# Gather order in a routed expert layer: V rows behind U rows, query products and index products

## The chip, the cores and the metric

The kernel runs on one core of a Trainium2 chip. The metric is the time on the device in microseconds (us), lower is better. Five engines run side by side, each through its own instructions in order, and wait for one another by semaphores: TensorE (matrix products; PE in the profile), VectorE (DVE), ScalarE (ACT), GpSimd (POOL) and SyncE (SP). In this kernel GpSimd issues the indirect DMA gathers and SyncE the plain loads.

## The reference

Two networks in a row on 256 tokens of width 1024. The first has two layers; each is a mixer (attention and pooling) and then the expert part, which is all that the change touches:

```python
def one_block(xblk):                      # 128 tokens
    q = (xblk @ w_query).reshape(B, TOKEN_BLOCK, N_PEER_HEADS, 2, SUBKEY_DIM)
    s = jnp.einsum('bthpd,hpnd->bthpn', q, sub_keys).astype(jnp.float32)
    vals, idx = lax.top_k(s, PEER_TOPK)
    cand = ...                            # 16 x 16 sums of the two halves
    top_s, pos = lax.top_k(cand, PEER_TOPK)
    eidx = jnp.take_along_axis(cand_idx, pos, axis=-1)
    g = jax.nn.softmax(top_s, axis=-1).astype(xblk.dtype)
    u = expert_u[eidx]
    h = jnp.einsum('btd,bthkd->bthk', xblk, u)
    act = jax.nn.gelu(h, approximate=False) * g
    return jnp.einsum('bthk,bthkd->btd', act, expert_v[eidx])
```

There are 8 heads, 16 experts per token and head, and 16384 experts, each with a row of 1024 floats in U and one in V. Every layer so reads 256 x 8 x 16 rows of U and as many of V, 268 MB in all. The second network (four dense layers) is not touched.

## The kernel before, in words

**Chunks.** A chunk is one head for one tile of 128 tokens; there are 16 (NCH), in the order of CHUNKS: heads 0 and 1 on tile 0, heads 0 and 1 on tile 1, then heads 2 to 7, each on tile 0 and tile 1. Chunk 4 is the first of head 2, chunk 8 the first of head 4.

**GpSimd** (line 2767 on) issues the gathers, one queue, strictly in order. `u_rows(c, g)` gathers group g of chunk c: four DMAs of 128 rows (512 KB each) into four of 8 buffers; it waits for the chunk's expert indices and for the dots that free the buffers (two groups back). `v_rows(q)` gathers set s = q % 4 of chunk c = q // 4, also four DMAs, into buffers that belong to the set; it waits until TensorE has summed the same set of the chunk before (`v_free`), and set 0 also for the chunk's indices by pair (`it_used`). U groups and V sets alternate: V set q follows U group q + VLAG, VLAG = 2. V rows are laid out by pair: a DMA takes the rows of 8 x 16 pairs of token and expert, not of one expert place for 128 tokens, and so needs its indices in another order than U.

**VectorE** (line 2385 on) works through `dots(c)`: 16 dots of a token's row with a U row (line 2454), about 1.15 us each. Between them it makes the expert lists of a later chunk, in four parts (`topk_part`): part 0 copies the head's scores out of PSUM (lines 2390, 2394), part 3 ends with the indices (line 2429) and with "indices spread" (line 2433, semaphore `ri_ready`), from which TensorE makes the indices by pair. From chunk 3 on, the dots of chunk c carry the parts of chunk c + 2, part 3 behind the last dot. The start differs: the dots of chunk 1 carry the parts of chunk 2 (behind dots 8 and 12), and the dots of chunk 2 carry those of chunk 3 (parts 0 and 1 behind dot 4, parts 2 and 3 behind dot 8) and of chunk 4 (behind dots 12 and 16). At the end of a chunk's dots VectorE spreads the weights (line 2466), copies the indices by pair of the next chunk (`take_indices`, line 2443), and then `stationaries(c)` (line 2479) writes the columns of expert weights that TensorE uses as stationary operand ("columns" below, semaphore `wst_ready`). Then come the dots of chunk c + 1.

**TensorE** (line 1073 on) does per chunk: `weights_by_pair` (line 1126, "weights product"), then `expert_sum(c)`: four sets of V rows times the columns (line 1141), each waiting for its rows to land. The product for the indices by pair of chunk c + 2 (`indices_by_pair`, line 1118, "index product", waits for `ri_ready`) lies ahead of set 2. Into six of the chunks (ASKED: chunk to head) the work on a later head is woven: `query_keys` (line 1084, "keys": four transposes of the head's sub keys, behind the copy of the scores of the head before, and in chunk 1 behind the copy at line 2390), `query_rows` parts 0 to 3 (line 1097, two halves of 16 products in the code, 32 in the trace) and `key_scores` (line 1108, "scores"). Before: keys ahead of the columns of set 0 (in chunk 1 behind set 0), parts 0 and 1 behind set 0, parts 2, 3 and scores behind set 1.

**ScalarE** copies keys and query halves out of PSUM between two chunks' gates. **SyncE** loads the query weights of head h (2 MB) when the query of head h - 2 is done.

## Time and profile before

| | us |
|---|---|
| median of 3 runs | 3297.96 |
| lowest and highest | 3285.51, 3304.04 |
| span of the profiled execution | 3263.7 |

The time of the profiled execution itself is not listed beside the three; its span, from the first to the last instruction, is 34.3 us below the median. Shares of the span are averages over stages of different kind: the expert part of layer 0 lies between about 241 us (first gather) and 1019 us, that of layer 1 between about 1230 us and 2008 us, and the rest is dense work. In rows of the trace, the first number is the start in us, the second how long it took, then engine, line, operation, tiles and count; in brackets is the idle time of the engine just before and what ended it. "issue" means that the profile shows nothing that was waited for, "remote" a releaser that it doesn't know. A product of TensorE has two records where the data are 32-bit floats, so a set of 8 products reads x16. Its ends are modelled, and a record may lie well ahead of the release that follows from it.

### The profile page before, as it was taken

To read this page: it belongs to the slowest core of one execution; us is meant where nothing else is said; L and a number is where in the kernel's file an instruction comes from. 1 tells how busy PE (TensorE), PEld (TensorE's weight loads), DVE (VectorE), ACT (ScalarE), POOL (GpSimd) and SP (SyncE) were. 2 spreads that over 40 slices of the span, in tenths; PEclk is the share of its full clock that TensorE was granted. 3 is DMA by queue.
4 is the path that set the end of the run, shared out by engine and by line. 5 is a ranking of instruction groups with operands and counts; after the bars stand their busy time and mean duration, and the time that the engine had idled before them with its cause. 6 is when DMAs were issued, how large, how long until landed. Compare 5 with 4: busy or idle time off the path is not lost.

```text
span 3263.7 us, 34887 instructions
## 1 busy us (share of the span) xinstructions
PE 2431.9 (75%) x12607; PEld 1727.6 (53%) x12607; DVE 2088.5 (64%) x4416; ACT 933.8 (29%) x1486; POOL 1043.1 (32%) x1060
## 2 busy tenths in 40 slices
PE   5996555544546997555545545999999999999998
PEld 4754422221103764422221102789879988997797
DVE  7878576666656958576666654655555555556654
ACT  3511011110112421011101112544554446445543
POOL 0105566666663105566566663100010001000000
PEclk9998777766667998677666766989999999999999
DMA  9858999999999839999999998345534542554353
GB/s 363 299 209 332 353 374 380 378 379 365 361 378 341 295 139 342 350 370 394 377 359 372 356 365 307 131 143 191 180 130 155 180 168 82 190 194 155 110 193 123
DMA packets 308642, 886.31 MB, mean 272 GB/s; under 512 B 22824, under 2 KB 32144, under 8 KB 308240
## 3 DMA queue, kind: packets, MB, share of 16 engines
q0 software_dynamic: 147456, 536.94, 42.9%
q1 hardware_dynamic: 161040, 347.51, 29.9%
q8 instruction: 82, 1.34, 0.2%
q14 instruction: 64, 0.52, 0.0%
HBM read 883.32 MB, written 1.05 MB: 271 GB/s over the span
## 4 chain that ended last, share of the span: by engine, by line
PE 46%; issue 31%; DVE 9%; another core or an unknown queue 6%; DMA 4%; SPq 2%; ACT 2%; POOL 1%; DVEq 0%; ACTq 0%; POOLq 0%
PE lin L837 7%; PE lin L838 7%; PE lin L839 7%; PE psT L839 2%; PE psT L838 2%; PE psS L838 2%; PE psS L839 2%; PE psT L837 2%; PE psS L837 2%; PE lin L1141 2%; PE psS L1097 2%; PE psS L887 2%; DMA ring<-in_w_in 2%; PE lin L1014 1%
## 5 line engine op out<-in xcount | busy, mean ns | idle before, releaser
L2454 DVE CUSTOM_DVE_ANT_0 proj<-proj,psT 128x1024 f32<-128x1024 f32 x512 | 606.1, 1218 | 211.1 <-DMA proj<-in_expert_u,eidx 120.5
L1928 DVE TENSOR_TENSOR weights_split<-ring,weights_split 128x1024 fp32r<-128x1024 f32 (+1 forms) x360 | 431.5, 1207 | 376.2 <-ACT weights_split L1712 373.6
L2787 POOL DMA_INDIRECT proj<-in_expert_u,eidx x512 | 481.5, 940 | 424.7 <-DVEq L2430 212.7
L1712 ACT ACTIVATE weights_split<-ring 128x1024 fp32r<-128x1024 f32 (+1 forms) x376 | 391.5, 1046 | 467.7 <-PE lin L839 291.6
L1141 PE MATMUL lin<-vbuf,rowb 128*32 128x512 f32 x1024 | 252.0, 879 | 266.8 <-issue 180.4
L2823 POOL TENSOR_TENSOR weights_split<-ring,weights_split 128x1024 fp32r<-128x1024 f32 x16 | 37.9, 2376 | 995.3 <-ACT weights_split L1712 995.3
L1141 PE MATMUL lin<-ring,rowb 128*32 128x512 f32 x896 | 208.8, 755 | 153.1 <-issue 107.1
L837 PE MATMUL lin<-weights_split,xT_high 128*128 128x512 f32 (+1 forms) x736 | 295.0, 401 | 19.6 <-issue 8.2
L839 PE MATMUL lin<-weights_split,xT_high 128*128 128x512 f32 (+1 forms) x736 | 288.1, 391 | 0.0
L2800 POOL DMA_INDIRECT ring<-in_expert_v,pT x224 | 211.0, 942 | 231.4 <-remote 86.8
L2800 POOL DMA_INDIRECT vbuf<-in_expert_v,pT x256 | 241.2, 942 | 115.5 <-issue 76.5
L1141 PEld LDWEIGHTS lin<-vbuf,rowb 128*32 128x32 f32 x1024 | 45.3, 136 | 422.5 <-issue 320.6
L1644 ACT ACTIVATE gel<-hdot 128x16 f32<-128x16 f32 x32 | 6.9, 215 | 771.3 <-DVE hdot L2454 450.1
L1097 PE MATMUL psS<-xT,ring 128*128 128x256 f32 x768 | 197.3, 415 | 32.8 <-issue 22.3
L1097 PEld LDWEIGHTS psS<-xT,ring 128*128 128x128 f32 x768 | 158.5, 210 | 93.3 <-issue 58.0
L837 PE MATMUL lin<-weights_split,act_split 128*128 128x512 f32 x512 | 200.1, 391 | 0.0
L838 PE MATMUL lin<-weights_split,act_split 128*128 128x512 f32 x512 | 199.5, 390 | 0.0
L839 PE MATMUL lin<-weights_split,act_split 128*128 128x512 f32 x512 | 199.2, 389 | 0.0
L1141 PEld LDWEIGHTS lin<-ring,rowb 128*32 128x32 f32 x896 | 39.4, 128 | 284.2 <-issue 226.7
L838 PE MATMUL lin<-weights_split,xT_low 128*128 128x512 f32 (+1 forms) x480 | 186.8, 389 | 0.0
L837 PEld LDWEIGHTS lin<-weights_split,xT_high 128*128 128x128 f32 x736 | 142.5, 194 | 55.5 <-issue 21.1
L839 PEld LDWEIGHTS lin<-weights_split,xT_high 128*128 128x128 f32 x736 | 142.5, 194 | 29.0
(336 smaller groups left out, 4943.9 us busy)
## 6 DMA issues: line engine op xcount, KB each, us to landing
ring<-in_mlp_w_up SPq DMA_DIRECT2D x32, 2048.0 KB, 8.1
ring<-in_mlp_w_down SPq DMA_DIRECT2D x32, 2048.0 KB, 7.9
ring<-in_w_in SPq DMA_DIRECT2D x14, 2048.0 KB, 14.1
ring<-in_w_query SPq DMA_DIRECT2D x14, 2048.0 KB
vbuf<-in_ada_w SPq DMA_DIRECT2D x12, 2048.0 KB, 12.9
ring<-in_diff_w_in SPq DMA_DIRECT2D x11, 2048.0 KB, 8.1
proj<-in_ada_w SPq DMA_DIRECT2D x24, 512.0 KB, 5.1
ring<-in_moba_w_in SPq DMA_DIRECT2D x6, 2048.0 KB, 8.0
```

The source lines that it names most:

```text
L837: pe.matmul(out_ap, lhs[0], rhs[0], start=first, stop=False, skip_group_check=True)
L838: pe.matmul(out_ap, lhs[1], rhs[0], start=False, stop=False, skip_group_check=True)
L839: return pe.matmul(out_ap, lhs[0], rhs[1], start=False, stop=last, skip_group_check=True)
L887: mm = pe.matmul(psS[:, g % 2, t * S:t * S + n], qkT[lo:hi, qb, t * P:(t + 1) * P], qkT[lo:hi, kb, 0:n], start=True, stop=True)
L1097: mm = pe.matmul(psS[:, 1, (b % 2) * S:(b % 2 + 1) * S], query_weights(h)[:, k, b * P:(b + 1) * P], xT[:, k, :], start=(k == 0), stop=(k = ...
L1141: mm = pe.matmul(lin[32 * b:32 * b + 32, 2 * half + t, :], wst[:, c % 2, 4 * b + s, :], vrow(SETROWS * s + b)[:, half * 512:(half + 1) * 5 ...
L1712: act.activation(part(p, 0, kind, w), raw_piece(slot, p, kind, w), ACT.Copy).then_inc(hi_ready, 1)
L1928: dve.tensor_tensor(part(p, 1, kind, w), raw_piece(slot, p, kind, w), part(p, 0, kind, w).bitcast(F32), ALU.subtract).then_inc(lo_ready, 1)
L2454: dve.tensor_tensor_reduce(ubuf[:, n % GB, :], ubuf[:, n % GB, :], x_row, 1.0, 0.0, ALU.mult, ALU.add, hdot[:, cb, k:k + 1]).then_inc(h_re ...
L2787: pool.indirect_dma_start(out=ubuf[:, (16 * c + k) % GB, :], out_offset=None, in_=table["u"], in_offset=bass.IndirectOffsetOnAxis(ap=eidx[ ...
L2800: pool.indirect_dma_start(out=vrow(SETROWS * s + b), out_offset=None, in_=table["v"], in_offset=bass.IndirectOffsetOnAxis(ap=eidxT[:, c % ...
L2823: pool.tensor_tensor(part(p, 1, "flat", D), raw_piece(o_slot, p, "flat", D), part(p, 0, "flat", D).bitcast(F32), ALU.subtract).then_inc(lo ...
```

## The change

Four edits, all in the order of work; no product, copy or DMA is added or removed.

1. `indices_by_pair(c + 2)` goes from ahead of set 2 to ahead of set 0, in chunks 1 to 13.
2. ASKED: heads 4 to 7 are worked on in chunks 3, 5, 7, 9 in place of 4, 6, 8, 10. In these the keys, parts 0 and 1 lie behind set 1, and parts 2, 3 and scores behind set 2. In chunks 1 and 2 (heads 2 and 3) keys, parts 0 and 1 lie behind set 0 and the rest behind set 1; so for chunk 2 only the keys move, from ahead of set 0 to behind it.
3. V rows follow the U rows by three groups for chunks 4 to 14, and by two as before for chunks 0 to 3 and 15.
4. The call of `query_keys` outside `expert_sum` goes.

```diff
-ASKED = {1: 2, 2: 3, 4: 4, 6: 5, 8: 6, 10: 7}
+ASKED = {1: 2, 2: 3, 3: 4, 5: 5, 7: 6, 9: 7}
+LAGS = [2] * (2 * NT) + [3] * (NCH - 2 * NT - 1) + [2]
...
                     pe.wait_ge(wst_ready, c + 1)
+                    if 0 < c < NCH - 2:
+                        indices_by_pair(c + 2)
                     for s in range(NSET):
-                        if s == 2 and 0 < c < NCH - 2:
-                            indices_by_pair(c + 2)
...
-                        if c in ASKED and s < 2:
-                            if c == 1 and s == 0:
+                        if c in ASKED:
+                            if s == (0 if c < 3 else 1):
                                 query_keys(ASKED[c])
-                            query_rows(ASKED[c], 2 * s)
-                            query_rows(ASKED[c], 2 * s + 1)
-                            if s == 1:
+                                query_rows(ASKED[c], 0)
+                                query_rows(ASKED[c], 1)
+                            if s == (1 if c < 3 else 2):
+                                query_rows(ASKED[c], 2)
+                                query_rows(ASKED[c], 3)
                                 key_scores(ASKED[c])
...
                     weights_by_pair(c)
-                    if c in ASKED and c > 1:
-                        query_keys(ASKED[c])
                     expert_sum(c)
...
+                q = 0
+                for c in range(NCH):
                     for g in range(4):
                         u_rows(c, g)
-                        if 4 * c + g >= VLAG:
-                            v_rows(4 * c + g - VLAG)
+                        while q < NSET * NCH and q + LAGS[q // NSET] <= 4 * c + g:
+                            v_rows(q)
+                            q += 1
```

TensorE's order in chunk 1 of a layer, before: the weights product (line 1126), set 0 (vbuf), keys, half of the query, set 1 (ring), the other half, scores, and only then the index product (line 1118).

```order
L1126 MATMUL psS<-const,pT 128x16 [waits indices_by_pair_copied,weights_spread]
L1141 MATMUL lin<-vbuf,rowb 32x512 [waits v_set_landed0,expert_weight_columns_ready]
L1141 MATMUL lin<-vbuf,rowb 32x512 x7
L1084 MATMUL psS<-const,ring 128x128 [waits peer_query_copied,sub_keys_copied,first_tile_scores_copied,sub_keys_loaded0]
L1084 MATMUL psS<-const,ring 128x128 x3
L1097 MATMUL psS<-xT,ring 128x256 [waits sub_keys_copied,query_slot_loaded1]
L1097 MATMUL psS<-xT,ring 128x256 x15
L1141 MATMUL lin<-ring,rowb 32x512 [waits v_set_landed1]
L1141 MATMUL lin<-ring,rowb 32x512 x7
L1097 MATMUL psS<-xT,ring 128x256 [waits peer_query_copied]
L1097 MATMUL psS<-xT,ring 128x256 x15
L1108 MATMUL psS<-pT,sm 128x128 [waits peer_query_copied]
```

The same place now; the lines are one or more further on in the file (1127 is the weights product, 1119 the index product).

```order
L1127 MATMUL psS<-const,pT 128x16 [waits indices_by_pair_copied,weights_spread]
L1119 MATMUL psS<-const,pT 128x16 [waits indices_spread,expert_weight_columns_ready]
L1142 MATMUL lin<-vbuf,rowb 32x512 [waits v_set_landed0]
L1142 MATMUL lin<-vbuf,rowb 32x512 x7
L1085 MATMUL psS<-const,ring 128x128 [waits peer_query_copied,sub_keys_copied,first_tile_scores_copied,sub_keys_loaded0]
L1085 MATMUL psS<-const,ring 128x128 x3
L1098 MATMUL psS<-xT,ring 128x256 [waits sub_keys_copied,query_slot_loaded1]
L1098 MATMUL psS<-xT,ring 128x256 x15
L1142 MATMUL lin<-ring,rowb 32x512 [waits v_set_landed1]
```

The index product, with its wait for the spread indices, stands ahead of set 0 and of all that follows it.

GpSimd's order at the start of chunk 4, now (proj is a U group, ring, pr and vbuf are V sets; each group is one row with its waits and one for the other three DMAs).

```order
L2788 DMA proj<-in_expert_u,eidx 128x1024 [waits expert_dots_ready]
L2788 DMA proj<-in_expert_u,eidx 128x1024 x3
L2801 DMA vbuf<-in_expert_v,pT 128x1024 [waits v_set_free]
L2801 DMA vbuf<-in_expert_v,pT 128x1024 x3
L2788 DMA proj<-in_expert_u,eidx 128x1024 [waits expert_dots_ready]
L2788 DMA proj<-in_expert_u,eidx 128x1024 x3
L2788 DMA proj<-in_expert_u,eidx 128x1024 [waits expert_dots_ready]
L2788 DMA proj<-in_expert_u,eidx 128x1024 x3
L2801 DMA vbuf<-in_expert_v,pT 128x1024 [waits v_set_free,indices_by_pair_copied]
L2801 DMA vbuf<-in_expert_v,pT 128x1024 x3
L2788 DMA proj<-in_expert_u,eidx 128x1024 [waits expert_dots_ready,expert_indices_ready]
L2788 DMA proj<-in_expert_u,eidx 128x1024 x3
```

Before, every U group was followed by a V set, and set 0 of a chunk came behind U group 2 of it, as in these rows of before.

```order
L2787 DMA proj<-in_expert_u,eidx 128x1024 [waits expert_dots_ready]
L2787 DMA proj<-in_expert_u,eidx 128x1024 x3
L2800 DMA vbuf<-in_expert_v,pT 128x1024 [waits v_set_free,indices_by_pair_copied]
L2800 DMA vbuf<-in_expert_v,pT 128x1024 x3
L2787 DMA proj<-in_expert_u,eidx 128x1024 [waits expert_dots_ready]
L2787 DMA proj<-in_expert_u,eidx 128x1024 x3
L2800 DMA ring<-in_expert_v,pT 128x1024 [waits v_set_free]
L2800 DMA ring<-in_expert_v,pT 128x1024 x3
```

Two U groups now follow one another once, and from there on set 0 comes behind U group 3.

## Rows read from the trace of the kernel before

**Rows 1.** The page: span, and busy time of each engine.

```profile
span 3263.7 us, 34887 instructions
...
PE 2431.9 (75%) x12607; PEld 1727.6 (53%) x12607; DVE 2088.5 (64%) x4416; ACT 933.8 (29%) x1486; POOL 1043.1 (32%) x1060
```

**Rows 2.** Stretches: length, busy PE PEld DVE ACT POOL, clock, DMA share, GB/s.

```profile
600.00:620.00 20.00, 13.26 (x43) 7.48 (x40) 14.32 (x37) 0.00 (x0) 15.12 (x17) 0.76 1.03 410
720.00:740.00 20.00, 16.93 (x108) 10.50 (x109) 12.51 (x33) 5.98 (x8) 12.27 (x14) 0.95 0.81 280
444.00:956.00 512.00, 257.48 (x1134) 103.49 (x1137) 332.42 (x832) 54.17 (x81) 330.44 (x353) 0.69 0.97 375
1428.00:1943.00 515.00, 268.19 (x1130) 106.50 (x1129) 332.36 (x829) 53.27 (x80) 329.80 (x353) 0.68 0.97 373
```

**Rows 3.** Waits of GpSimd, 444 to 956 us: total, times, longest.

```profile
POOL ring L2800 <- PE lin L1141: 38.3, 9, 8.2
POOL ring L2800 <- remote: 32.4, 7, 5.9
```

**Rows 4.** Timeline of TensorE, chunk 1 of layer 0.

```profile
362.87 1.92 PE L1141 MATMUL lin<-vbuf,rowb 128*32 128x512 f32 x16 [0.78 <-DVE rowb L2479]
368.08 1.09 PE L1084 MATMUL psS<-const,ring 128*128 128x128 f32 x4 [3.29 <-issue]
369.94 9.16 PE L1097 MATMUL psS<-xT,ring 128*128 128x256 f32 x32 [0.78 <-ACT pT L1617]
...
398.29 0.29 PE L1118 MATMUL psS<-const,pT 128*128 128x16 f32 x2
```

**Rows 5.** Timeline of VectorE, chunks 2 and 3 of layer 0.

```profile
367.50 0.42 DVE L2390 COPY rope_t<-psS 128x256 f32<-128x256 f32 x1
...
383.99 0.29 DVE L2433 TENSOR_TENSOR pT<-posfl,prow 128x128 f32<-128x128 f32 x1 [0.16 <-issue]
...
398.49 0.69 DVE L2394 COPY rope_t<-psS 128x512 f32<-128x512 f32 x1 [9.64 <-PE psS L1108]
...
416.64 0.68 DVE L2479 TENSOR_TENSOR rowb<-const,psS 128x512 f32<-128x512 f32 x1
...
450.12 0.17 DVE L2443 CAST pT<-psS 128x16 uint32<-128x16 f32 x1 [5.16 <-remote]
```

**Rows 6.** Timeline of TensorE, chunk 1 of layer 1.

```profile
1345.84 3.64 PE L1141 MATMUL lin<-vbuf,rowb 128*32 128x512 f32 x16 [0.78 <-DVE rowb L2479]
1350.85 1.09 PE L1084 MATMUL psS<-const,ring 128*128 128x128 f32 x4 [1.37 <-issue]
```

**Rows 7.** Timeline of VectorE, chunk 2 of layer 1.

```profile
1366.75 0.29 DVE L2433 TENSOR_TENSOR pT<-posfl,prow 128x128 f32<-128x128 f32 x1 [0.16 <-issue]
...
1381.87 0.69 DVE L2394 COPY rope_t<-psS 128x512 f32<-128x512 f32 x1 [10.27 <-PE psS L1108]
```

**Rows 8.** Timeline of TensorE, chunks 8 and 9 of layer 0.

```profile
695.27 6.96 PE L1097 MATMUL psS<-xT,ring 128*128 128x256 f32 x31
...
731.25 0.29 PE L1118 MATMUL psS<-const,pT 128*128 128x16 f32 x2
...
753.97 3.62 PE L1141 MATMUL lin<-vbuf,rowb 128*32 128x512 f32 x10 [8.43 <-DMA vbuf<-in_expert_v,pT]
...
779.85 0.58 PE L1126 MATMUL psS<-const,pT 128*128 128x16 f32 x2 [9.27 <-DVE pT L2443]
```

**Rows 9.** Timeline of VectorE: the columns of chunks 8 and 9.

```profile
691.24 0.68 DVE L2479 TENSOR_TENSOR rowb<-const,psS 128x512 f32<-128x512 f32 x1
...
737.09 0.68 DVE L2479 TENSOR_TENSOR rowb<-const,psS 128x512 f32<-128x512 f32 x1
```

**Rows 10.** Timeline of GpSimd, chunks 9 and 10 of layer 0.

```profile
721.20 0.94 POOL L2800 DMA_INDIRECT ring<-in_expert_v,pT  x1 [8.16 <-PE lin L1141]
722.44 0.94 POOL L2800 DMA_INDIRECT ring<-in_expert_v,pT  x1 [0.30 <-issue]
...
779.08 0.94 POOL L2800 DMA_INDIRECT ring<-in_expert_v,pT  x1 [3.83 <-remote]
```

3 lines of the change are left out of this document (1 added, 2 removed).

## The prediction

> **What bounds the kernel now.** I read first the page's engines and span [rows 1]: no engine is busy all the time, so the answer is by stage. The change touches only the expert part of the two mixing layers, so I read that stage by its stretches [rows 2]. From chunk 4 to chunk 14 it takes 512 us in layer 0 and 515 us in layer 1; DMA is busy at 0.97 there and moves 375 and 373 GB/s, against 410 GB/s in the best 20 us. So the pace is set near the transfers, but not by them alone: 512 x 375 GB/s is 192 MB, which at 410 would take 468 us, 44 us less; in layer 1 it is 46 us less. Then the waits of GpSimd, which issues the gathers [rows 3]: in those 512 us it waits 38.3 us for TensorE's expert sums before V rows, and another 32.4 us before the same V rows for a releaser that the profile calls remote. Last, instruction by instruction, the places that the edits move: chunk 1 on TensorE and VectorE [rows 4, 5, 6, 7] and the pair of chunks 8 and 9 [rows 8, 9, 10]. There the reader is to see who stands in front of whom in TensorE's queue.
>
> **The index product ahead of set 0, chunk 1.** In every chunk from 2 on this costs nothing: the product for chunk c+2 waits for "indices spread", which VectorE posts at the end of its dots of chunk c, just ahead of the columns without which set 0 can't start anyhow. In chunk 1 the order is another. The lists of chunk 3 are made in the dots of chunk 2, behind the eighth dot, and the diff puts TensorE's wait for them in front of sum 0 of chunk 1. In the trace that sum starts at 362.87 [rows 4]; VectorE makes the spread indices of chunk 3 at 383.99 + 0.29 = 384.28 [rows 5]. With the index product (0.4, an estimate from the 0.29 to 0.58 of such products) set 0 starts near 384.7. TensorE has then stood idle 22 us, so I price the set with its long form, 3.64 us in layer 1, not the short 1.92 of layer 0 [rows 4, 6]: it ends at 388.3.
>
> Queued behind it on TensorE are keys, query, set 1, query, and scores of head 2. Before, the keys began at 368.08, held only by a copy on VectorE at 367.50 [rows 4, 5]. Now they begin at 388.3: **20.2 us later**. VectorE needs the scores of head 2 in the middle of its dots of chunk 2: it waited 9.64 us for them and copied them at 398.49 [rows 5]; now at 418.7. Its last four dots, the columns at 416.64 and the dots of chunk 3 come later by as much. The U rows of chunk 3 are asked for when dots of chunk 2 free their buffers, so GpSimd can't run ahead and fill this hole. Layer 1 repeats it: 1366.75 + 0.29 + 0.4 + 3.64 = 1371.1 against 1350.85 is again 20.2, and VectorE again waited there, 10.27 us [rows 6, 7]. Bounds: 18.5 per layer if set 0 runs in its short form, 28 if the query after the idle time runs as slowly as in chunk 8, where it takes 731.25 - 695.27 = 36.0 us against 398.29 - 369.94 = 28.4 [rows 4, 8]. I take 20.2, since the rows of the place itself give it; below nothing it can't go, for nothing in the new order starts sooner there. Two layers: **+40.4**.
>
> On the speed of TensorE after a pause, the row shows 3.64 us against 1.92 for the same 16 products. The Trainium skill (TensorE: Matmul & The Clock Gate, "HAM oscillation — how this bites in real kernels") says that an array left idle between bursts is throttled again and starts each burst cold. The trace agrees, with a mean granted clock of 0.69 and 0.68 in the two stretches [rows 2]. By that rule the whole query of head 2, not only set 0, could start at 1.2 GHz, which is the 28 us end above; by the row of the place it is 20.2.
>
> **Keys behind set 0, chunk 2.** Before, the keys (4 transposes) and their copy lay ahead of set 0, under VectorE's work; now they lie behind it: 369.94 - 368.08 = 1.9 us [rows 4]. Against that, VectorE waited 5.16 us at 450.12 for the index product, which stood behind the scores [rows 5]; that wait goes, but the columns that follow also need TensorE's next weights product, which stands behind sets 2 and 3 as before. So of the 5.16 I count only as much as the keys cost: between -3.3 and +1.9, taken as 0.
>
> **Queries at chunks 3, 5, 7, 9 behind sets 1 and 2.** The number of products is the same; head 4 is asked for one chunk sooner, so the scores are never late. In the chunk that holds a query TensorE is the long queue: columns to columns is 691.24 to 737.09, 45.9 us, and in it set 0, query, set 1, query, scores, set 2, set 3 stand one behind the other [rows 8, 9]. The keys join this queue: +1.9 us in 4 chunks, 7.4 us per layer, as an upper bound of loss. What is gained: sets 0 and 1 come free before the query and not between its halves. Set 1's release held GpSimd 8.16 us before the gather at 721.20 [rows 10]. In 720 to 740 us the rate is 280 GB/s instead of 410, so 6.3 us of transfer time are lost [rows 2]. Four such chunks: at most 25 us per layer.
>
> **V rows one U group later, chunks 4 to 14.** Nothing is added; a group of four U and four V gathers is 8 x 1.24 = 9.9 us of GpSimd, so each V set is asked for about 10 us later, more than the longest wait of 8.16. These waits should go. But each set also lands 10 us later, and set 3 must be summed before TensorE can take the next chunk's weights. In chunk 9, set 3 starts when its rows land, at 753.97, after 8.43 us of waiting; GpSimd is let go at 779.08 and the next weights follow at 779.85 [rows 8, 10]. There is no slack of 10 us there, so a good part of the gain passes from GpSimd's wait into VectorE's. Bounds per layer for the two edits together: 44 us of gain (all transfers at 410) and 7.4 us of loss (keys only). I take **5 us of gain**: the 25 us of the query chunks less 7.4, and of the remaining 17 about a third, because what frees the gathers (779.08) and what frees the weights (779.85) come together. Two layers: **-10**. This is the least certain term.
>
> At the end of the layer chunk 15 keeps its lag; one U group moves 5 us back, but the last V set, which ends the layer, stays last. Nothing is counted.
>
> **The sum** is made against the profiled span of 3263.7 [rows 1]: +40.4 - 10 = +30.4, so 3294.1. The median of the three runs, 3297.96, lies 34.3 above the span, and I carry that over: **3328 us**. About 0.5% (16.5 us) is what a measurement of this kernel can tell from no change.
>
> **Rivals.**
> 1. Forecast (0.50): chunk 1 holds, the middle gives 0 to 12 us a layer: 3314 to 3340, likeliest 3328.
> 2. The lag pays half of the ceiling, 22 us a layer: 3298 + 40.4 - 44 = 3294, no measurable change (0.25, 3285 to 3310). For it speak 71 us of GpSimd's waits in layer 0 [rows 3]; against it the place at 779, where sums and weights come free together.
> 3. Faster (0.12): the transfers get the pace to themselves. One mechanism: with V rows off GpSimd's critical place, the middle stretch runs near 410 GB/s. It decides from 20.2 + 8.3 = 28.5 us of gain a layer, which is 192 MB in 483.5 us, or 397 GB/s in the stretch that had 375. At 35 us a layer the time is 3268. For it: 410 is reached for 20 us at a time; against it: queries still fill 46 us of TensorE.
> 4. Clearly slower (0.13): the query of head 2 starts cold (28 instead of 20.2) and the keys cost 7.4 without any gain: 35.4 a layer, 3369 at its end, 3350 in its middle.
> That the edit doesn't act as named is no rival for the index product, since the order of the instructions shows it; what could be false is only that its lists are late, and rows 5 and 7 say that they are.
>
> **How the numbers follow.** Forecast 3328. Slower by over 0.5% (above 3314.5): nearly all of case 1 and case 4, 0.60. Within 0.5%: case 2 and the low edge of case 1, 0.28. Faster (under 3281.5): 0.12. The range leaves out the lower part of case 3 and the upper part of case 4: 3280 to 3355. The cases on the slow side alone: 3312 to 3355.
>
> **What would show it.** In the profile after: set 0 of chunk 1 starts right behind the spread indices of chunk 3, about 22 us behind its columns; VectorE's wait for the scores of head 2 grows from 9.64 to near 30 us, in both layers; the dots of chunk 3 begin near 437 instead of 417. If that wait stays under 15 us, the first term is wrong. For the middle: the waits of GpSimd in [rows 3] go under 30 us together, the stretch from chunk 4 to chunk 14 shrinks by about 5 us and its rate stays under 385 GB/s, and VectorE waits longer for the weights product. A rate of 397 or more would make the forecast wrong on the fast side; a stretch longer than 512 us, on the slow side.

## The result, and the profile after

The changed kernel takes **3435.78 us** (median of 4 runs, 3420.42 to 3439.53) against 3299.82 us for the kernel before beside it (4 runs, 3285.51 to 3304.04): 1.0407 times, interval 1.0379 to 1.0435, 136 us more. The forecast was 3328 with a range to 3355. The direction was right, the size was not: 30 us were forecast and four and a half times as much came.

The profiled run took 3437.78 us and its span is 1.9 us less. So the 34.3 us between span and median that the prediction carried over were no fixed overhead; the execution that was profiled before was one of the quicker ones of that kernel, and differences between the two traces can be some 30 us too large over the whole span. The page answers to [rows 1]:

```profile
span 3435.9 us, 34897 instructions
...
PE 2359.2 (69%) x12607; PEld 1728.2 (50%) x12607; DVE 2086.0 (61%) x4416; ACT 935.0 (27%) x1486; POOL 1046.9 (30%) x1060
```

The work is the same, the idle time is not. The same stretch as in [rows 2], from the first gather of chunk 4 to the first of chunk 15, in both layers:

```profile
468.00:1029.00 561.00, 226.70 (x1118) 101.32 (x1116) 329.00 (x820) 51.58 (x77) 327.92 (x349) 0.67 0.88 337
1531.00:2103.00 572.00, 236.92 (x1134) 106.58 (x1132) 328.22 (x822) 54.12 (x80) 328.36 (x349) 0.67 0.86 331
```

It has grown by 49 and 57 us, and the rate has fallen from 375 and 373 GB/s to 337 and 331. The rest of each layer grew too: from its first gather to that of chunk 4 by 24 us in layer 0 and 14 in layer 1, and from the first gather of chunk 15 to the last of the layer by 11 and 8. The waits of GpSimd in the stretch of layer 0, which answer to [rows 3] (total, times, longest):

```profile
POOL proj L2788 <- DVE hdot L2455: 106.0, 10, 18.5
...
POOL ring L2801 <- remote: 20.0, 5, 5.6
```

The 70.7 us that GpSimd waited for V buffers (both rows of [rows 3]) are down to some 20: what the lag was for, it did. In their place GpSimd waits 106.0 us for dots of VectorE, where it waited 0.9 us before. And VectorE waits for the gelu of ScalarE; first the kernel before in its stretch, then the changed one:

```profile
DVE actw L2464 <- ACT gel L1644: 16.7, 7, 7.8
```

```profile
DVE actw L2465 <- ACT gel L1645: 105.1, 4, 31.0
```

**Chunk 1** looks as forecast. TensorE, layer 0 (answers to [rows 4]), then VectorE (answers to [rows 5]; the first row is the columns of chunk 1):

```profile
394.44 0.58 PE L1119 MATMUL psS<-const,pT 128*128 128x16 f32 x2 [22.24 <-DVE pT L2434]
394.95 3.64 PE L1142 MATMUL lin<-vbuf,rowb 128*32 128x512 f32 x16
398.53 1.10 PE L1085 MATMUL psS<-const,ring 128*128 128x128 f32 x4
400.41 7.14 PE L1098 MATMUL psS<-xT,ring 128*128 128x256 f32 x32 [0.78 <-ACT pT L1618]
...
417.20 2.05 PE L1109 MATMUL psS<-pT,sm 128*128 128x128 f32 x16 [0.69 <-issue]
```

```profile
372.24 0.69 DVE L2480 TENSOR_TENSOR rowb<-const,psS 128x512 f32<-128x512 f32 x1 [21.93 <-PE psS L1127]
...
421.72 0.69 DVE L2395 COPY rope_t<-psS 128x512 f32<-128x512 f32 x1 [22.86 <-remote]
...
439.89 0.68 DVE L2480 TENSOR_TENSOR rowb<-const,psS 128x512 f32<-128x512 f32 x1
```

Set 0 stands 22 us behind its columns, in its long form of 3.64 us, at a granted clock of 0.50 (the lower level, 1.2 GHz). The wait for the scores is 22.86 us where some 30 were forecast.

**The middle** is another matter. Chunk 9 has a query, chunk 10 none. TensorE (each row with x1 is one product alone), then ScalarE, which copies the two halves of the query and then makes the gelu of chunk 10, then VectorE, then GpSimd:

```profile
808.73 7.14 PE L1098 MATMUL psS<-xT,ring 128*128 128x256 f32 x32 [1.53 <-ACT const L1618]
...
823.61 1.01 PE L1142 MATMUL lin<-ring,rowb 128*32 128x512 f32 x1 [1.52 <-issue]
826.39 1.01 PE L1142 MATMUL lin<-ring,rowb 128*32 128x512 f32 x1 [1.78 <-issue]
...
843.97 10.16 PE L1098 MATMUL psS<-xT,ring 128*128 128x256 f32 x32 [10.96 <-ACT sm L1630]
...
858.65 0.40 PE L1127 MATMUL psS<-const,pT 128*128 128x16 f32 x2
```

```profile
843.32 0.60 ACT L1630 ACTIVATE sm<-psS 128x512 f32<-128x512 f32 x1 [34.73 <-remote]
854.16 0.60 ACT L1630 ACTIVATE sm<-psS 128x512 f32<-128x512 f32 x1 [10.25 <-PE psS L1098]
...
856.07 0.22 ACT L1645 ACTIVATE gel<-hdot 128x16 f32<-128x16 f32 x1
```

```profile
856.39 0.23 DVE L2465 SCALAR_TENSOR_TENSOR actw<-eg,ers,gel 128x16 f32<-128x16 f32 x1 [31.04 <-ACT gel L1645]
```

```profile
837.21 0.94 POOL L2788 DMA_INDIRECT proj<-in_expert_u,eidx  x1 [0.30 <-issue]
843.71 0.94 POOL L2801 DMA_INDIRECT ring<-in_expert_v,pT  x1 [5.56 <-remote]
```

The first half of the query begins at 808.73 and its records end at 815.9, but ScalarE gets it at 843.32, 27 us later. Meanwhile set 2 of the same chunk trickles: one product every 2.1 to 2.8 us, with nothing that the profile shows as waited for. The copy comes only when GpSimd has stopped issuing: last gather at 837.21, copy at 843.32. GpSimd's next gather follows at 843.71, so it too got what it waited for at that moment; which of the two let the other go, these rows don't tell.

VectorE has the same thing at the end of chunk 11, in the small instructions that make an expert list, each of which needs the one before. First the kernel before, behind chunk 8, then the changed one:

```profile
687.40 0.43 DVE L2423 TENSOR_TENSOR xn<-posfl,const 128x256 f32<-128x256 f32 x1
687.86 0.42 DVE L2424 TENSOR_TENSOR xn<-xn,idxf 128x256 f32<-128x256 f32 x1
```

```profile
893.89 0.42 DVE L2425 TENSOR_TENSOR xn<-xn,idxf 128x256 f32<-128x256 f32 x1 [0.31 <-DVE xn L2424]
895.29 0.42 DVE L2426 TENSOR_REDUCE posfl<-xn 128x16 f32<-128x256 f32 x1 [0.98 <-DVE xn L2425]
896.70 0.48 DVE L2424 TENSOR_TENSOR xn<-posfl,const 128x256 f32<-128x256 f32 x1 [0.98 <-DVE posfl L2426]
```

The same instructions, 0.46 us apart before and 1.4 us apart now, with no one in between. The end of a chunk (last dot to first dot of the next, the chunk's tail from here on) takes 18 us behind chunk 11; behind chunk 8 of the kernel before it took 6, and 6 to 14 behind its chunks 4 to 14. In layer 0 tails of 18 us stand behind chunks 5, 7, 9, 11 and 13, tails of 35 to 37 us, which hold the gelu wait, behind 6, 8 and 10, and tails of 21 and 24 us behind 4 and 12.

### The profile page after: what moved, and what is told of

Read it like the earlier page. It is cut to its first block, busy times and chain, and to the rows that moved or that the text cites. A ratio compares the mean times of both kernels' runs of the same rounds, so it can differ in the third digit from the quotient of the medians.

```text
span 3435.9 us, 34897 instructions
## 1 busy us (share of the span) xinstructions
PE 2359.2 (69%) x12607; PEld 1728.2 (50%) x12607; DVE 2086.0 (61%) x4416; ACT 935.0 (27%) x1486; POOL 1046.9 (30%) x1060
## 3 DMA queue, kind: packets, MB, share of 16 engines
q1 hardware_dynamic: 161040, 347.51, 28.4%
## 4 chain that ended last, share of the span: by engine, by line
PE 45%; DVE 17%; another core or an unknown queue 14%; issue 11%; POOL 4%; DMA 4%; ACT 3%; SPq 2%; DVEq 0%; POOLq 0%; ACTq 0%
PE lin L838 7%; PE lin L839 7%; PE lin L840 7%; DVE proj L2455 5%; POOL proj L2788 2%; PE psS L1098 2%; PE lin L1015 2%; DMA proj<-in_expert_u,eidx 2%; PE psT L840 2%; PE psT L839 2%; PE psS L839 2%; PE psS L840 2%; PE psT L838 2%; PE psS L838 2%
## 5 line engine op out<-in xcount | busy, mean ns | idle before, releaser
L1142 PE MATMUL lin<-vbuf,rowb 128*32 128x512 f32 x1024 | 196.3, 884 | 228.5 <-DMA vbuf<-in_expert_v,pT 186.3
L1119 PE MATMUL psS<-const,pT 128*128 128x16 f32 x64 | 16.6, 337 | 313.9 <-issue 168.4
L1142 PE MATMUL lin<-ring,rowb 128*32 128x512 f32 x896 | 170.1, 678 | 64.6 <-issue 60.1
L1142 PEld LDWEIGHTS lin<-vbuf,rowb 128*32 128x32 f32 x1024 | 36.5, 140 | 320.6 <-DMA vbuf<-in_expert_v,pT 202.4
L1119 PEld LDWEIGHTS psS<-const,pT 128*128 128x128 f32 x64 | 13.9, 271 | 318.3 <-issue 222.8
L838 PEld LDWEIGHTS lin<-weights_split,xT_high 128*128 128x128 f32 x736 | 143.1, 194 | 53.4 <-issue 20.5
```

The lines of the kernel that those rows point to most:

```text
L838: pe.matmul(out_ap, lhs[0], rhs[0], start=first, stop=False, skip_group_check=True)
L1142: mm = pe.matmul(lin[32 * b:32 * b + 32, 2 * half + t, :], wst[:, c % 2, 4 * b + s, :], vrow(SETROWS * s + b)[:, half * 512:(half + 1) * 5 ...
```

## The experiments

Each ratio is to the kernel before on the same chip. The chips differ, which turned out to matter: on chips 13 and 15 the kernel before takes 3285 to 3296 us, close to the comparison above (whose chip isn't listed), on chips 9 and 2 it takes 3140 us. These two are called the quick chips from here on. The changed kernel itself ran in the first comparison (1.0407, interval 1.0379 to 1.0435) and on chip 2 (after_again), not on 13, 15 or 9; differences to it across chips carry the uncertainty of both ratios, some 15 to 20 us.

| kernel | chip | us | ratio, 95% interval |
|---|---|---|---|
| index_only | 15 | 3320.67 | 1.0081, 1.0051 to 1.0111 |
| lag_only | 15 | 3349.50 | 1.0169, 1.0138 to 1.0199 |
| query_only | 15 | 3334.62 | 1.0138, 1.0094 to 1.0182 |
| after_index1_back | 15 | 3399.27 | 1.0324, 1.0293 to 1.0355 |
| after_pause | 9 | 3284.60 | 1.0457, 1.0440 to 1.0475 |
| after_gelu | 9 | 3159.15 | 1.0061, 1.0044 to 1.0078 |
| after_sets01 | 9 | 3158.56 | 1.0059, 1.0042 to 1.0076 |
| before_again | 9 | 3135.05 | (one run) |
| after_again | 2 | 3156.73 | 1.0052, 1.0035 to 1.0069 |
| after_pause14 | 2 | 3228.61 | 1.0282, 1.0265 to 1.0299 |
| after_gelu2 | 2 | 3160.14 | 1.0062, 1.0045 to 1.0079 |
| after_sets01b | 2 | 3156.72 | 1.0058, 1.0040 to 1.0075 |
| after_half_v | 13 | 3410.37 | 1.0381, 1.0337 to 1.0425 |
| after_pause14b | 13 | 3448.63 | 1.0491, 1.0448 to 1.0534 |
| after_gelu3 | 13 | 3397.76 | 1.0323, 1.0277 to 1.0368 |
| after_index1_b | 13 | 3392.24 | 1.0311, 1.0264 to 1.0359 |
| after_break | 13 | 3384.55 | 1.0299, 1.0272 to 1.0327 |
| index1_breaks | 13 | 3384.23 | 1.0293, 1.0261 to 1.0325 |

### One edit at a time

The first three kernels are the kernel before with one part of the diff that stands ahead; the fourth is the changed kernel with this:

```diff
-                    if 0 < c < NCH - 2:
+                    if 1 < c < NCH - 2:
                         indices_by_pair(c + 2)
                     for s in range(NSET):
+                        if c == 1 and s == 2:
+                            indices_by_pair(3)
```

> The kernel before with edit 1 alone: the index product ahead of set 0 in chunks 1 to 13. The trace of the changed kernel shows chunk 1 as predicted in kind: set 0 of chunk 1 starts at 395 us (363 before), the dots of chunk 3 at 440 us (417 before), about 22 us late in each layer. Theory 1 (the loss of chunk 1 is paid in full, elsewhere the edit is free): 3300 + 40 to 44 = 3340 to 3344 us. Rival (the delay is absorbed behind chunk 3, since GpSimd catches up while transfers have room): under 3315 us. Second rival (the edit costs in every chunk): the whole loss of 136 us sits here, 3436 us.

> The kernel before with edit 3 alone: V rows three U groups behind in chunks 4 to 14. In the changed kernel GpSimd issues 14 gathers without a pause across nearly every end of a chunk's dots, at 410 GB/s, and in every second chunk VectorE's list of small instructions there takes 18 us instead of 5 us. Theory A (the lag makes these long runs of gathers, and the small instructions are slow in them): the loss that is not chunk 1's, 136 - 44 = 92 us, sits here, about 3390 us, with tails of 15 us and more. Theory B (the loss comes from the query, whose copies on ScalarE hold the gelu of the next chunk): the lag alone gains what the prediction gave it or more, 3256 to 3300 us.

> The kernel before with edit 2 (and 4) alone: queries in chunks 3, 5, 7, 9 behind sets 1 and 2. Theory B (in the changed kernel VectorE waits 31.0 us for the gelu of chunk 10, which stands on ScalarE behind the copies of head 7's query; four such waits in a layer): most of the 92 us, about 3390 us, with waits of VectorE for the gelu of over 20 us in chunks 6, 8, 10. Theory A: no such waits without the lag, 3295 to 3315 us.

> The changed kernel with the index product of chunk 1 alone put back ahead of set 2; all the rest as changed. Theory 1: the loss of chunk 1 comes back in full, 3436 - 44 = 3392 us, and the dots of chunk 3 begin near 417 us. Rival (the middle of the layer is bound by its own pace and the delay was absorbed): within 10 us of 3436 us.

Costs in us are worked out from the ratios. The index product alone costs 27 us (17 to 37), and putting it back in chunk 1 alone gives back 1.0407 - 1.0324 = 27 us: theory 1 in kind, two thirds of its price. The lag alone costs 56 us (45 to 66), the query alone 46 (31 to 60). The three sum to 0.0388 against 0.0407 measured, so within what the intervals can tell they add up, and theories A and B both hold a half. B's gelu waits (layer 0, 468 to 1029 us) come with either edit; first lag_only, then query_only:

```profile
DVE actw L2465 <- ACT gel L1645: 41.6, 3, 20.0
```

```profile
DVE actw L2464 <- ACT gel L1644: 58.0, 3, 19.6
```

And A's slow lists come with either as well: tails of 12 to 25 us with 4 to 12 slow steps stand in both kernels, in five or six chunks of a layer. In index_only one tail has four, no other more than one.

### Pause, gelu, sets, and a second trace of before

> The changed kernel with one more wait of GpSimd: set 0 of V rows of chunks 4 to 13 is asked for only when the dots of that chunk are done, a pause of some 6 us (chunk 11: gather at 881.8, dots done at 888.4) that the 10 us of transfers already asked for cover. In the six traces so far, small instructions of VectorE's list that follow within 20 us of the start of an unbroken run of gathers come 0.05 us after one another, those 24 us and more after it 0.9 to 1.3 us. Theory P (it is the unbroken run of GpSimd that slows them): the run starts anew at the end of the dots, the 18 us tails behind chunks 5, 7, 9, 11, 13 shrink to 6 us, and with them the time: 3436 - 10 x 12 = 3316 us if nothing else takes over, 3380 us if the next wait takes half of it. Theory D (it is the transfers at 410 GB/s that slow them): the transfers go on through the pause, the tails stay at 16 us or more, and the time is 3436 us or above.

```diff
                     if s == 0:
                         pool.wait_ge(it_used, c + 1)
+                        if 4 <= c < 14:
+                            pool.wait_ge(h_ready, 16 * c + 16)
```

> The changed kernel with ScalarE's order changed in the query chunks 3, 5, 7, 9: the gelu of the next chunk ahead of the two copies of the query halves. Theory B1 (VectorE's 31.0 us wait for the gelu of chunk 10 is ScalarE's order): the wait goes, four or five a layer of 20 to 30 us each, 3436 - 150 = 3280 us at best, certainly under 3380 us. Theory B2 (TensorE is late itself: the weights product, which VectorE needs for the next columns, stands behind the same query and ran at 858.65, 2.3 us after the gelu): VectorE then waits as long at the columns, and the time stays within 15 us of 3436 us.

```diff
-                def query_copies(h):
+                def query_copies(h, between=None):
                     keys_copy(h)
+                    if between is not None:
+                        hidden_gelu(between)
...
-                        query_copies(ASKED[c])
+                        query_copies(ASKED[c], c + 1 if c >= 3 else None)
```

> The changed kernel with the query halves back behind sets 0 and 1 in chunks 3, 5, 7, 9 (keys behind set 0); the chunks, the lag and the index product as changed. Theory B3 (the place behind sets 1 and 2 is what makes the query end late, 54 us after the columns in chunk 9 where it was 40 us): most of the query's share of the loss, about 40 of 46 us, comes back, 3396 us. Rival (the chunks are what matters, not the sets): within 10 us of 3436 us, and sets 1 waiting for the query hold GpSimd again for 5 to 8 us each.

```diff
-                            if s == (0 if c < 3 else 1):
+                            if s == 0:
...
-                            if s == (1 if c < 3 else 2):
+                            if s == 1:
```

> The kernel before, unchanged, for a second trace: the profiled execution of before had a span of 3263.7 us, 34 us under the median of its timed runs, and those of the edits alone lie within 21 us of theirs. If the execution profiled first was a quick one of several kinds, this span is nearer to 3296 us, and a chunk of it shows where executions of one kernel differ (the dots of chunk 1 begin at 363 us there and at 372 us in four of the others). If it is the profile that makes the span short, it is 3264 us again.

These ran on chip 9, and there the question was gone: no list instruction is slow in any of the four traces. before_again shows what the chips differ in. TensorE in chunk 1 of layer 0, the query of head 1 on tile 1, 64 records; first the trace that [rows 4] is from, then before_again:

```profile
330.21 5.96 PE L1059 MATMUL psS<-xT,ring 128*128 128x128 f32 x39
338.34 0.27 PE L1059 MATMUL psS<-xT,ring 128*128 128x128 f32 x1 [2.17 <-issue]
341.14 0.37 PE L1059 MATMUL psS<-xT,ring 128*128 128x128 f32 x1 [2.53 <-issue]
...
356.54 3.58 PE L1059 MATMUL psS<-xT,ring 128*128 128x128 f32 x16 [1.03 <-issue]
```

```profile
326.28 9.65 PE L1059 MATMUL psS<-xT,ring 128*128 128x128 f32 x64
```

The same instructions at the same place: 9.65 us on chip 9, 29.9 us (330.21 to 360.12) on the other, where nine come singly. So the trickle was in the kernel before too. It costs there as well: the tail behind chunk 1, which holds it, takes 28.5 us in both layers of the first trace and 8.5 in those of before_again. after_pause takes 1.0457 times before; GpSimd waits 8 to 14 us in each chunk and not 6, and the rate is 354 GB/s between 440 and 900 us, so the transfers run dry. The changed kernel itself, as the base for these, ran with three more on chip 2, which proved to be quick too:

> The changed kernel, unchanged, as the base for the three beside it. On the chip of the last four runs the kernel before took 3140 us instead of 3297, and not one of VectorE's small list instructions there came slowly, even 100 us into an unbroken run of gathers. Theory P' (the slow instructions belong to the chip, and they are most of the lag's and the query's cost): where before takes near 3140 us, this kernel takes 1.010 times before or less (chunk 1's delay of 27 us at most); where before takes near 3297 us, 1.04 times. Rival (the order itself costs 4% anywhere): 1.04 times before on either chip.

> The changed kernel with a shorter pause than in after_pause: set 0 of V rows waits for the 14th dot of its chunk and not for all 16, some 4 us after where it is asked for now (chunk 11: 881.8, 14th dot done at 885.8), so the 10 us of transfers already asked for bridge it. On a chip with slow list instructions, theory P (an unbroken run of GpSimd slows them, a pause starts it anew): the tails behind odd chunks go from 18 to 6 us, and the time is 60 us or more below after_again. Theory D (the transfers at 410 GB/s slow them): tails as before, and time as after_again or above. On a chip without slow instructions both say: nothing gained, 0 to 80 us lost.

> The same kernel as after_gelu, beside the changed kernel itself. Where VectorE's waits for the gelu are 31 us (chip with slow instructions): theory B1 (ScalarE's order) 150 us below after_again, theory B2 (TensorE is late itself) within 15 us of it. On the quick chip after_gelu ran at 1.0061 times before with waits of VectorE of 10 us in the chunks behind a query; there theory B1 expects after_again at 1.015 or more, B2 at 1.006.

> The same kernel as after_sets01, beside the changed kernel itself: query halves behind sets 0 and 1. On the quick chip it ran at 1.0059 times before, without a wait over 3 us in the ends of chunks 5 to 13. Theory B3 (the place behind sets 1 and 2 costs): after_again is at least 15 us slower on the quick chip and 30 us on the slow one. Rival (the place is worth nothing, the chunks are): within 8 us of after_again on either.

after_pause14 is after_pause with 14 dots in place of 16. On this chip the whole change costs **0.5%** (16.8 us): theory P' holds in its numbers, and the rival (4% anywhere) falls. Neither the gelu's place (B1) nor the sets (B3) is worth anything there, all three being within 4 us; on chips 13 and 15 B3 was not tried. The same stretch, chunk 4 to 15 of layer 0; first before_again (chip 9), then after_again (chip 2):

```profile
414.00:890.00 476.00, 196.05 (x1096) 92.08 (x1088) 337.01 (x833) 51.79 (x78) 331.81 (x352) 0.70 1.03 408
```

```profile
433.00:896.00 463.00, 223.55 (x1101) 94.02 (x1100) 331.35 (x821) 52.25 (x78) 328.47 (x348) 0.70 1.03 408
```

Both run at 408 GB/s, so there the transfers bind in both. The first gather of chunk 4 came 19 us later (414 to 433), that of chunk 15 only 6 us later (890 to 896). The 13 us between are not a higher rate, but 5 MB less in the stretch (189 against 194). Of these, 2.1 MB are the four V gathers (348 against 352 instructions of GpSimd) that the longer lag leaves behind the first gather of chunk 15, and they are paid at the end of the layer: from that gather to the last one it takes 55 us in place of 49. Layer 1 repeats it: 16 us later at chunk 4, 12 us given back, 4 more at the end. So on the quick chips each term has the sign that was forecast for it, but for the end of the layer. Columns to columns of chunks 1 and 2 grow by 18.3 and 17.5 us where 20.2 were forecast. And the first half of chunk 9's query, which took 34.6 us above, is handed over 7 us after its start at 717.69:

```profile
724.87 0.60 ACT L1630 ACTIVATE sm<-psS 128x512 f32<-128x512 f32 x1 [7.33 <-PE psS L1098]
```

### Transfers or GpSimd

Where the slow instructions exist, what do they go with? In nine traces of chips 13, 15 and of the first comparison (all but after_half_v and the two with breaks) I took each step between two instructions of the second half of VectorE's list (`topk_part` 2 and 3 without their searches for the 16 largest) that fell while GpSimd was issuing, and sorted it by the age of GpSimd's run (time since its last gap of over 1 us). A step is slow where it leaves over 0.25 us:

```
age of GpSimd's run     chips with slow steps     chips 9 and 2 (8 traces)
under 20 us             1739 steps,  1% slow      1755 steps, 0% slow
20 to 24 us               84 steps, 13% slow       135 steps, 0% slow
over 24 us               706 steps, 97% slow       901 steps, 0% slow
```

With the searches counted too, the same nine traces give 1% slow of 6704 steps under 20 us and 80% of 850 over 24 us, and the quick chips none of 2613 over 24 us. The age is a strong sign, but not the whole rule: in the kernel before, index_only and after_pause14b (below), 158 of the 197 steps at an age over 24 us are quick. Nor are long runs new. Runs of 39 us and more stand 8 times in the trace of the kernel before and 14 times in that of the changed one. What moved is where the list falls: of the steps sorted in the table 7 of some 300 lay at an age over 24 us before, and over 110 of some 220 do now.

The rate cannot be told apart from the age there, since old runs move some 410 GB/s. Hence the next four, on chip 13:

> The changed kernel with V rows gathered at half width: 256 KB in place of 512 KB for each of the V gathers (the first half of rows of half the length; TensorE uses that half twice), as many gathers as before, each still 1.24 us of GpSimd. So the transfers can take no more than (512 + 256) KB in 2.48 us, 317 GB/s, and no longer 410, while GpSimd's runs stay unbroken. On a chip with slow instructions (before near 3297 us): theory P (GpSimd's unbroken run) expects VectorE's list instructions still 1 us apart beyond 20 us of a run, and tails of 18 us; theory D (transfers at full rate) expects none slow, tails of 6 us, and a time under 3200 us. On a chip without slow instructions both expect tails of 6 us.

```diff
-"v": T["expert_v"].rearrange("l e d -> (l e) d")
+"v": T["expert_v"].rearrange("l e (a d) -> (l e a) d", a=2)
...
-                                               vrow(SETROWS * s + b)[:, half * 512:(half + 1) * 512]
+                                               vrow(SETROWS * s + b)[:, 0:512]
...
-                            out=vrow(SETROWS * s + b), out_offset=None
+                            out=vrow(SETROWS * s + b)[:, 0:512], out_offset=None
```

> The same kernel as after_pause14 (on the quick chip 1.0282 times before, 72 us more than the changed kernel). Where before takes near 3297 us: theory P expects tails of 6 us behind odd chunks and a time at or below 1.02 times before, less than the 1.04 of the change, though it adds a wait; theory D expects tails of 16 us and more where the transfers go on at 410 GB/s, and 1.04 or above. Where before takes near 3140 us: 1.028 again.

> The same kernel as after_gelu (gelu of the next chunk ahead of the copies of the query halves). Where before takes near 3297 us: theory B1 (ScalarE's order makes the 31 us waits) expects under 1.01 times before; theory B2 (TensorE's own queue is late, the weights product stands behind the query) expects 1.035 to 1.045, with the wait moved from the gelu to the columns. Where before takes near 3140 us: 1.006 again.

> The same kernel as after_index1_back (index product of chunk 1 put back ahead of set 2). On the chip where before takes near 3297 us it was 1.0324 times before, 27 us below the change. Where before takes near 3140 us, theory 1 (chunk 1's delay is all that the change costs without slow instructions) expects 0.997 to 1.001 times before; rival (there the gathers bind and absorb chunk 1's delay, the 0.5% come from the lag or the query) expects 1.004 to 1.006.

after_half_v settles the rate. The tail behind chunk 5 (fields as in [rows 2]), and VectorE in it:

```profile
563.10:581.00 17.90, 0.58 (x2) 0.50 (x2) 5.28 (x18) 2.81 (x5) 13.50 (x14) 0.50 0.89 309
```

```profile
567.50 0.18 DVE L2422 CAST posfl<-posu 128x32 f32<-128x32 uint32 x1 [1.22 <-DVE posu L2421]
568.22 0.42 DVE L2424 TENSOR_TENSOR xn<-posfl,const 128x256 f32<-128x256 f32 x1 [0.54 <-DVE posfl L2422]
569.61 0.43 DVE L2425 TENSOR_TENSOR xn<-xn,idxf 128x256 f32<-128x256 f32 x1 [0.97 <-DVE xn L2424]
```

At 309 GB/s the steps are as slow as at 410, the tail is 18 us again, and of this kernel's steps at an age over 24 us 95% are slow. A quarter of the bytes less, and the whole kernel takes 1.038 times before in place of 1.041, no difference within the intervals. Theory D falls as it was put: neither the slow steps nor the time hang on the rate. What this run keeps is the number of gathers and that the transfers go on without a break, so it does not tell GpSimd's issuing from those.

after_pause14b shows the other half. The tails behind chunks 5, 7, 9, 11 and 13 are 9.4 to 9.9 us in place of 18, none of their steps is slow (3 to 4 us of each are a wait for U rows, since the transfers had drained). The short tails of P are there, its price is not: the kernel takes 1.049 times before. The tails of 35 us behind chunks 6, 8 and 10 stay, and GpSimd now waits 5 to 14 us in every chunk ahead of set 0. Against P's rule stands that the searches of this kernel that fall 26 us into a run are quick as well: of 82 steps over 24 us 2 are slow. The pause lets both GpSimd's run and the transfers start anew, so this run does not tell these two apart either.

after_gelu3 speaks for B2, nearly: 1.0323, just under B2's 1.035 and far from B1's 1.01, about 27 us better than the 1.0407 of the change. VectorE's wait for the gelu is down to 8.6 us. In its place the columns wait for TensorE, and the list behind chunks 6, 8 and 10, quick in the changed kernel, has 10 of 12 steps slow:

```profile
DVE rowb L2483 <- PE psS L1127: 50.6, 4, 14.6
...
DVE actw L2468 <- ACT gel L1647: 8.6, 4, 7.8
```

after_index1_b repeats chunk 1's part on another chip: 1.0311 beside 1.0324.

### A break that waits for nobody

> The changed kernel, and ahead of set 0 of V rows in chunks 4 to 13 GpSimd clears 128x1024 numbers of unused memory twice, one after the other: a break in the issuing of some 2 us that waits for no other engine, bridged by the 10 us of transfers already asked for. In the traces, a gap of GpSimd of 1.5 us or more was enough for a new age of the run. Where before takes near 3297 us: theory P (the age of GpSimd's run) expects tails of 6 us behind chunks 5, 7, 9, 11, 13 in place of 18, shorter queries, and 1.00 to 1.02 times before in place of 1.04; the rival (the age only goes along with something else, such as how far VectorE and TensorE are behind) expects tails of 18 us and 1.04 or above. Where before takes near 3140 us both expect 1.005 to 1.015.

```diff
+                    if s == 0 and 4 <= c < NCH - 1:
+                        done = 2 * (10 * l + c - 4)
+                        for i in range(2 if c < NCH - 2 else 0):
+                            pool.wait_ge(rest_done, done + i)
+                            pool.memset(xn[:, 0, :], 0.0).then_inc(rest_done, 1)
+                        if c == NCH - 2:
+                            pool.wait_ge(rest_done, done)
```

> As after_break, with a second such break ahead of set 2 in the same chunks, so that no run of gathers gets older than about 20 us, and with the index product of chunk 1 back ahead of set 2. Where before takes near 3297 us: theory P expects no slow list instruction at all between chunks 4 and 13 and a chunk of about 45 us (32 gathers of 1.24 us and two breaks of 2 us make 44), so 0.985 to 1.00 times before, the quickest of all on that chip; the rival expects 1.03 and above. Where before takes near 3140 us, GpSimd becomes the bound, 44 us in place of 41 a chunk, and both expect 1.01 to 1.03.

In after_break the break does to the tails what P says. Behind chunks 5, 7, 9, 11 and 13 of layer 0 they are 5.9 to 6.6 us, in place of 18 (in layer 1 the one behind chunk 13 keeps 19). The transfers went on through it, at 416 GB/s between 757 and 761 us and 393 in the 4 us behind. VectorE behind chunk 9:

```profile
767.52 0.18 DVE L2423 CAST posfl<-posu 128x32 f32<-128x32 uint32 x1
767.74 0.42 DVE L2425 TENSOR_TENSOR xn<-posfl,const 128x256 f32<-128x256 f32 x1
```

But the time comes to 1.030 times before, between the two forecasts: about 35 us come back, not 70 and more.

index1_breaks goes against P. No run of gathers between chunks 4 and 13 is older than 20 us there, and P expects no slow list instruction. Yet 58 of 840 steps are slow (searches counted). Behind chunk 13 of layer 0 the tail takes 24 us, with 11 of 12 list steps slow, most of them 9 to 19 us behind a break. GpSimd's break, then VectorE:

```profile
955.14 1.98 POOL L2805 MEMSET xn<- 128x1024 f32 x2
```

```profile
968.75 0.42 DVE L2427 TENSOR_TENSOR xn<-posfl,const 128x256 f32<-128x256 f32 x1 [0.53 <-DVE posfl L2425]
970.15 0.43 DVE L2428 TENSOR_TENSOR xn<-xn,idxf 128x256 f32<-128x256 f32 x1 [0.97 <-DVE xn L2427]
971.54 0.42 DVE L2429 TENSOR_REDUCE posfl<-xn 128x16 f32<-128x256 f32 x1 [0.96 <-DVE xn L2428]
```

So a break of 2 us does not always start the age anew, and how long the transfers have gone on without a break may count besides GpSimd's run: 57 of the 58 slow steps fall where the gathers' transfers had not stood still (under 40 GB/s in a quarter of a microsecond) for over 30 us. No run here separates the two.

The next thing late is TensorE's query, in the part of the run behind the break. TensorE and GpSimd in chunks 9 and 10 of after_break:

```profile
784.18 0.65 PE L1086 MATMUL psS<-const,ring 128*128 128x128 f32 x4
812.61 9.79 PE L1099 MATMUL psS<-xT,ring 128*128 128x256 f32 x32 [27.77 <-ACT const L1619]
```

```profile
806.47 0.94 POOL L2809 DMA_INDIRECT vbuf<-in_expert_v,pT  x1 [0.31 <-issue]
812.40 0.94 POOL L2789 DMA_INDIRECT proj<-in_expert_u,eidx  x1 [4.99 <-remote]
```

Four transposes at 784.18 are handed over at 811.87 (ScalarE's copy), 27 us later and 5.4 us behind GpSimd's last gather. index1_breaks has a second break 20 us behind the first, and still the keys of chunk 7 wait from 679.52 to 712.36, until GpSimd, with its last gather at 707.93, stands still for 3.66 us. So a break of 2 us ahead of the list was enough for VectorE's list in after_break, and was not enough for TensorE's hand-over, which came in each case 4.4 to 6.1 us behind a last gather: 843.32 behind 837.21, 717.59 behind 712.10 in the kernel before, 811.87 behind 806.47, 712.36 behind 707.93. The forecast of 0.985 to 1.00 for index1_breaks was wrong, and with 1.0293 it is no better than the changed kernel with chunk 1 put back alone. No kernel here beats the kernel before.

## Why the prediction was wrong, point by point

- **Index product in chunk 1, +20.2 us a layer.** Right in place and in kind, a third too dear: measured 27 us for both layers, not 40.4. From columns to columns of chunks 1 and 2 it is 439.89 - 372.24 = 67.7 us against 416.64 - 362.13 = 54.5, so 13.1 us, and 12 in layer 1. The failed step of this term is "the query follows as before, only later": from the start of the query to the end of its scores it takes 419.2 - 400.4 = 18.8 us, not 28.4 [rows 4]. Its second half, before and now:

```profile
385.44 9.96 PE L1097 MATMUL psS<-xT,ring 128*128 128x256 f32 x32 [4.48 <-ACT sm L1629]
```

```profile
409.34 7.17 PE L1098 MATMUL psS<-xT,ring 128*128 128x256 f32 x32
```

The wait of 4.48 us for ScalarE's copy of the first half is gone. The two halves take 7.1 and 7.2 us at a granted clock of 1.00 (2.4 GHz), where they took 9.2 and 10.0 at 0.78 and 0.71. Before, TensorE had idled 3.29 us ahead of the keys; now it worked on from 394.44 without such a gap. The 28 us bound, a cold query, was the wrong way round. By the rule of the Trainium skill that the prediction cites (TensorE: Matmul & The Clock Gate, "HAM oscillation — how this bites in real kernels"), the array would start cold; the trace agrees for set 0 (3.64 us again, clock 0.50) and not for the query. On the quick chips, where the same query goes from 21.9 only to 20.6 us, the term came to 18.3 and 17.5 us.

- **Keys behind set 0 in chunk 2, 0.** Nothing in the traces of index_only or query_only speaks against it; it was not measured by itself.
- **Queries and lag, -10 us.** This is the step that failed, for the number as a whole. Together they cost about 100 us (after_index1_back, which holds little else, lies 103 us above before), one by one 46 and 56. The prediction gave 7.4 us a layer as the most that these edits could lose. It reckoned the cost of moved work from its length elsewhere, and took it that a wait of GpSimd that goes away can only help. The waits for V buffers did go, 70.7 to 20 us, as the sign for the middle said ("under 30 us together"). But on these chips TensorE and VectorE got on in such breaks: the late hand-overs came 4.4 to 6.1 us into one. With them gone the tails and the hand-overs fall into the old part of a run, and 106 us come back in layer 0 as waits for dots. That these waits were what the two engines lived on is the reading that fits most rows; index1_breaks and after_pause14b show that it is not the whole rule.
- **End of the layer, 0.** Wrong too: from the first gather of chunk 15 to the last of the layer it takes 64.6 and 62.5 us in place of 53.9 and 54.5, so 11 and 8 us more in the two layers, and 6 and 4 on the quick chips. The four V gathers that now lie behind that first gather are 5 us of it.
- **The offset of 34.3 us** was right for a forecast against the median, by luck rather than by its reason: it is no fixed overhead, the profiled execution was a quick one; in its layer 0 the dots of chunk 1 begin at 296 us, against 306 to 308 in the changed kernel and the three single edits.
- **The rivals.** None was this one. The fourth named the right side, with a cold query as its mechanism and 35.4 us a layer as its end; the measured loss is 68 a layer. The sign "a stretch longer than 512 us" stood there as the one that would make the forecast wrong on the slow side, and it came: 561. Where the direction was right, that is chunk 1's term; the middle went the other way.
- **What the trace of before had shown.** TensorE's rows between 704.69 and 717 in the kernel before are single products 2.1 to 2.8 us apart, ended by "issue", and so are those at 754 to 770, of which [rows 8] shows the first. The prediction read 28.4 and 36.0 us for the same query as two durations, and never asked why one piece of work has two. It took the longer for a cold query, but the first half of it in chunk 8 ran at a granted clock of 1.00 (695 to 703 us); the time went in the single products of set 1 between the halves.

Shown are: the split by edits on the slower chips, that the slow steps stand nearly all in the old part of GpSimd's runs and do not hang on the rate, that in after_break a break takes them out of VectorE's tails, and that on the quick chips neither they nor more than 0.5% of loss exist. Argued, not shown, is that GpSimd's unbroken issuing is what slows the others: after_break speaks for it, index1_breaks against it as a rule by itself, and unbroken transfers or the number of gathers asked for were not varied apart from it. Open is the mechanism: what holds up other engines' instructions and hand-overs, why on some chips alone, and what break would be enough for TensorE. The Trainium skill (DMA: Bandwidth & Descriptors, "SWDGE vs HWDGE vs iDMA") says that GpSimd writes the descriptors of such transfers itself, into rings that lie in SBUF. No run here shows whether that is the link, and by that rule chips 9 and 2, where GpSimd also needs 1.24 us a gather, would be no different.

## What to carry to other kernels

When the same work has two durations in one trace, find out what the longer one stands beside before pricing a move; here 28 and 36 us of query were the first sign of a cost of 100. A wait on an engine that is not the bound can be time in which the others get on: before taking it away, look at what they do during it. A sorting of many steps by one variable shows where the slow ones are, not what makes them slow; the run that breaks the rule, here index1_breaks, is worth as much as the ones that fit. And run both kernels on more than one chip before calling an order good or bad: the same diff costs 0.5% on one (chip 2) and 4% on another.

## What the runs showed of the hardware that I had not expected

- On chips 13 and 15, small instructions of the second half of VectorE's list, which depend on one another, leave 1.04 us between them (mean of 706) where GpSimd has issued gathers for over 24 us without a gap of 1 us, and 0.05 us (mean of 1739) under 20 us. With the searches counted, 80% of 850 are slow in place of 97%. TensorE's products come singly, 1.4 to 2.8 us apart, and earlier in a run: from 16 us on in chunk 9 of the changed kernel (819.39, the run begins at 803.61), from 21 us on in chunk 8 of the one before (704.69, the run begins at 683.52). Its results are handed over up to 27 us late, in four cases 4.4 to 6.1 us behind GpSimd's last gather. The dots of VectorE, which wait for no result of VectorE's own, keep their 1.22 us in the old part of a run.
- On chips 9 and 2 the same programs show none of it, even where GpSimd has issued for over 100 us: 0 of 901 steps are slow. The kernel before takes 3140 us on both against 3285 to 3296, and moves 408 GB/s (before_again, chunks 4 to 14) where it moved 375.
- Halving the V rows (317 GB/s at most while gathers are issued) left the time where it was: 1.0381 times before on chip 13, against 1.0407 for the changed kernel in the first comparison.
